# State-space stage of a two-layer hybrid backbone: both directions' decay weights in one matrix, and another order of the blocks

## The reference

```python
def ssd_chunked(x, dt, A, B, C, init_state):
    ...
    acum = jnp.moveaxis(jnp.cumsum(dtc * A.reshape(G, HG), axis=2), 2, -1)
    causal = jnp.tril(jnp.ones((CHUNK, CHUNK), dtype=bool))
    seg = jnp.where(causal, acum[..., :, None] - acum[..., None, :], -jnp.inf)
    cb = jnp.einsum('bcign,bcjgn->bcgij', Cc, Bc)
    w_intra = cb[:, :, :, None] * jnp.exp(seg)
    dtx = xc * dtc[..., None]
    y_diag = jnp.einsum('bcghij,bcjghp->bcighp', w_intra, dtx)
    decay_to_end = jnp.exp(acum[..., -1:] - acum)
    chunk_states = jnp.einsum('bcghj,bcjgn,bcjghp->bcghpn', decay_to_end, Bc, dtx)
    ...
    y_off = jnp.einsum('bcign,bcghpn,bcghi->bcighp', Cc, S_in, jnp.exp(acum))
    y = (y_diag + y_off).reshape(b, L, SSD_HEADS, P)

    y_f, s_f = ssd_chunked(x, dt_f, A[0], B, C, init_f)
    y_b, s_b = ssd_chunked(x[:, ::-1], dt_b[:, ::-1], A[1], B[:, ::-1], C[:, ::-1], init_b)
    y = y_f + y_b[:, ::-1] + p['d_skip'].astype(jnp.float32)[:, None] * x.astype(jnp.float32)
```

## Time and profile before

| | us |
|---|---|
| median of 3 runs | 1587.03 (1586.55 to 1587.52) |
| the profiled execution | 1585.54 |
| its span in the profile | 1583.6 |
| PE busy | 1487.9 (94%) |
| DVE busy | 893.6 (56%) |
| ACT busy | 673.6 (43%) |
| POOL busy | 157.0 (10%) |

### The profile page before, as it was taken

How to read it: one execution, slowest core, us unless ns; L and a number is a source line. 1 busy time by engine, 2 the same in 40 slices (tenths; PEclk the granted TensorE clock), 3 DMA queues, 4 the chain that set the end, 5 groups by cost and what they waited for, 6 DMA issues and landing times.

```text
span 1583.6 us, 21312 instructions
## 1 busy us (share of the span) xinstructions
PE 1487.9 (94%) x8503; PEld 1355.5 (86%) x8503; DVE 893.6 (56%) x1453; ACT 673.6 (43%) x1148; POOL 157.0 (10%) x141
## 2 busy tenths in 40 slices
PE   6889798899999999999998897999999999999998
PEld 2779576888899999999987896777888999999997
DVE  2697354465456654554546974455644667555562
ACT  2534453435354533342435444445335455344351
POOL 0010200344000000000010102015320010000000
PEclk9899899999999999999999998999999999999999
DMA  9446563222334556565645341221324333433430
GB/s 322 149 133 213 158 204 94 67 85 76 108 119 135 171 186 202 166 221 173 211 152 159 94 110 54 81 67 54 115 72 139 115 120 120 132 121 121 131 121 40
DMA packets 186088, 210.21 MB, mean 133 GB/s; under 512 B 10702, under 2 KB 154374, under 8 KB 185990
## 3 DMA queue, kind: packets, MB, share of 16 engines
q1 hardware_dynamic: 185990, 208.86, 42.3%
HBM read 204.90 MB, written 3.93 MB: 132 GB/s over the span
## 4 chain that ended last, share of the span: by engine, by line
PE 84%; DVE 9%; ACT 3%; issue 2%; POOL 1%; DMA 1%; SPq 0%; DVEq 0%; ACTq 0%; POOLq 0%
PE bank L638 21%; PE bank L639 21%; PE bank L640 21%; PE y_ps L886 3%; PE bank L652 2%; PE bank L653 2%; PE bank L654 2%; DVE tb L1514 2%; DVE wlo L1418 1%; PE bank L670 1%; PE seg_ps L670 1%; PE seg_ps L776 1%; PE y_ps L908 1%; PE y_ps L895 1%; PE y_ps L792 1%
## 5 line engine op out<-in xcount | busy, mean ns | idle before, releaser
L1418 DVE TENSOR_TENSOR wlo<-raw,whi 128x1024 fp32r<-128x1024 f32 (+1 forms) x288 | 353.2, 1233 | 247.6 <-ACT whi L1049 246.2
L638 PE MATMUL bank<-ahi,whi 128*128 128x384 f32 (+1 forms) x1280 | 447.0, 349 | 6.4 <-DVE wlo L1418 6.4
L1049 ACT CAST whi<-raw 128x1024 fp32r<-128x1024 f32 (+1 forms) x288 | 296.4, 1036 | 337.0 <-PE bank L640 172.8
L639 PE MATMUL bank<-alo,whi 128*128 128x384 f32 (+1 forms) x1280 | 437.6, 342 | 0.0
L640 PE MATMUL bank<-ahi,wlo 128*128 128x384 f32 (+1 forms) x1280 | 436.9, 341 | 0.0
L638 PE MATMUL bank<-bhi,whi 128*128 128x384 f32 x768 | 262.8, 342 | 8.0 <-DVE arena_g L1623 4.7
L638 PEld LDWEIGHTS bank<-ahi,whi 128*128 128x128 f32 x1280 | 245.0, 191 | 21.2 <-issue 12.3
L639 PE MATMUL bank<-blo,whi 128*128 128x384 f32 x768 | 259.4, 338 | 0.0
L640 PE MATMUL bank<-bhi,wlo 128*128 128x384 f32 x768 | 259.4, 338 | 0.0
L639 PEld LDWEIGHTS bank<-alo,whi 128*128 128x128 f32 x1280 | 245.1, 191 | 3.2 <-issue 2.7
L640 PEld LDWEIGHTS bank<-ahi,wlo 128*128 128x128 f32 x1280 | 244.7, 191 | 0.0
(11 more groups left out here) (224 smaller groups left out, 1478.4 us busy)
## 6 DMA issues: line engine op xcount, KB each, us to landing
raw<-in_w_mlp_dram SPq DMA_DIRECT2D x128, 512.0 KB, 3.6
raw<-in_w_in_dram SPq DMA_DIRECT2D x104, 512.0 KB, 3.7
raw<-in_w_mod_dram SPq DMA_DIRECT2D x96, 512.0 KB, 6.4
raw<-in_w_ssd_o_dram SPq DMA_DIRECT2D x16, 512.0 KB, 3.4
raw<-in_w_out_dram SPq DMA_DIRECT2D x16, 512.0 KB, 3.4
raw<-in_w_pool_o_dram SPq DMA_DIRECT2D x8, 512.0 KB, 3.4
raw<-in_w_attn_o_dram SPq DMA_DIRECT2D x8, 512.0 KB, 3.4
raw<-in_w_in_dram SPq DMA_DIRECT2D x8, 256.0 KB, 3.0
```

The source lines that it names most:

```text
L638: nc.tensor.matmul(dst, uh[:, k, tm_cols(m)], hi[k0 + k], start=first and k == 0, stop=False)
L639: nc.tensor.matmul(dst, uh[:, k, tm_cols(m)], lo[k0 + k], start=False, stop=False)
L1049: nc.scalar.copy(dst, src).then_inc(hi_ready, 1)
L1418: nc.vector.tensor_tensor(rest, full, top.bitcast(F32), ALU.subtract).then_inc(lo_ready, 1)
```

## The change

One matrix per chunk and head serves both directions. Above the diagonal (and on it) it holds the forward differences, below it the backward ones. PE still makes both directions' seg matrices; ACT copies the forward one from `seg_ps` to `ew` (`seg_copy`), DVE's `pick`, a predicated copy with the new constant `after` as mask, puts the backward one over it where j > i, ACT's `seg_exp` takes one Exp, and DVE's `weigh` multiplies by `cbs`, which is now an unmasked copy. The factor dt is in the exponent: `log_slots`, the logarithm of dt with a minus, is added by six more products with the identity (at L850), so that `ydiag` multiplies `ew` by x itself, once per chunk, and `dtx_rows` goes. The backward direction's diagonal, which the one matrix lacks, goes with the skip term: `skip_columns` (DVE) makes dt_b times the diagonal of C B^T plus d_skip for each head, and `skip_rows` (POOL) multiplies x by it into `dtx`. `softplus` gets a max, a memset of `log_slots`, a second Ln on ACT and the write of `log_slots`. The order in a group changes on all four engines, and with it the slots (8 in place of 13).

```diff
-SSD_SLOTS = ((2, 1, 1, 0, 1, 0, 1, 0, 0, 1, 0, 1, 0), (1, 1, 1, 1, 1, 0, 1, 0, 0, 1, 0, 1, 0))
+SSD_SLOTS = ((2, 1, 1, 1, 1, 0, 1, 1), (1, 1, 1, 1, 1, 1, 1, 1))
```

The order of PE, and its new products:

```diff
-                    ins = nc.tensor.matmul(seg_ps[:, i // 4, tm_cols(i % 4)], adt_slots[:, tm_cols(i)], tri[i % 2], start=True, stop=True,
+                    ins = nc.tensor.matmul(seg_ps[:, i // 4, tm_cols(i % 4)], adt_slots[:, tm_cols(i)], tri[i % 2], start=True, stop=False,
+                                           skip_group_check=True)
+                    ins = nc.tensor.matmul(seg_ps[:, i // 4, tm_cols(i % 4)], log_slots[:, tm_cols(i)], ident, start=False, stop=True,
                                            skip_group_check=True)
...
+                def ydiag(g, t):
+
+                    pe.wait_ge(w_ready, (l * 2 + g) * 3 + t + 1)
+                    if t or g:
+                        pe.wait_ge(y_free, (l * 2 + g) * 3 + t)
                     for h in range(HG):
+                        ins = nc.tensor.matmul(ybank[:, h * 64:h * 64 + 64], ew[:, (g + t) % 2, h, :],
+                                               xbuf[:, t, (g * HG + h) * 64:(g * HG + h) * 64 + 64], start=h == 0, stop=h == 7,
+                                               skip_group_check=True)
...
                     transposes4(2, stage[:, 2])
-                    ydiag(g, 0, 0)
                     seg(g, 2)
                     fill(slot[2])
-                    ydiag(g, 0, 1)
+                    ydiag(g, 0)
                     state_sum(3, 2)
+                    seg(g, 3)
                     fill(slot[3])
                     state_sum(4, 1)
-                    seg(g, 3)
                     fill(slot[4])
+                    seg(g, 4)
                     state_sum(5, 0)
-                    ydiag(g, 1, 0)
-                    fill(slot[5])
+                    ydiag(g, 1)
                     pe.wait_ge(stT_ready, (l * 2 + g) * 2 + 1)
                     transposes4(6, stage[:, 0])
-                    seg(g, 4)
-                    fill(slot[6])
-                    ydiag(g, 1, 1)
+                    seg(g, 5)
                     state_sum(7, 0)
-                    fill(slot[7])
+                    fill(slot[5])
                     pe.wait_ge(stT_ready, (l * 2 + g) * 2 + 2)
                     transposes4(8, stage[:, 0])
-                    seg(g, 5)
-                    fill(slot[8])
-                    ydiag(g, 2, 0)
                     yoff(9, 1, 0, 0)
-                    fill(slot[9])
+                    fill(slot[6])
                     yoff(10, 1, 1, 3)
-                    fill(slot[10])
-                    ydiag(g, 2, 1)
+                    ydiag(g, 2)
                     yoff(11, 2, 0, 2)
-                    fill(slot[11])
+                    fill(slot[7])
                     yoff(12, 2, 1, 1)
```

ACT:

```diff
+                act.wait_ge(dt_step, l * 4 + 4)
+                nc.scalar.activation(dtw, dtm, ACT.Ln).then_inc(dt_act, 1)
...
+                def seg_copy(g, t):
+
+                    act.wait_ge(seg_done, (l * 2 + g) * 6 + 2 * t + 1)
+                    n = g * 3 + t
+                    if n >= 2:
+                        act.wait_ge(ydiag_done, l * 6 + n - 1)
+                    nc.scalar.copy(ew[:, (g + t) % 2].rearrange("p h i -> p (h i)"), seg_ps[:].rearrange("p b n -> p (b n)"))\
+                        .then_inc(seg_taken, 1)
+
+                def seg_exp(g, t):
+                    act.wait_ge(seg_taken, (l * 2 + g) * 6 + 2 * t + 2)
+                    rows = ew[:, (g + t) % 2].rearrange("p h i -> p (h i)")
+                    nc.scalar.activation(rows, rows, ACT.Exp).then_inc(exp_ready, 1)
...
+                    seg_copy(g, 0)
+                    keep(1, st[:, 0, :], st_ready, (l * 2 + g) * 2 + 1)
                     seg_exp(g, 0)
...
                     fill(slot[1])
                     keep(2, st[:, 1, :], st_ready, (l * 2 + g) * 2 + 2)
+                    seg_copy(g, 1)
+                    fill(slot[2])
+                    seg_exp(g, 1)
+                    fill(slot[3])
+                    fill(slot[4])
+                    seg_copy(g, 2)
+                    keep(5, stage[:, 0, :], stT_ready, (l * 2 + g) * 2 + 1)
+                    keep(6, stage[:, 1, :], state_staged, (l * 2 + g) * 2 + 1)
+                    keep(7, stage[:, 0, :], stT_ready, (l * 2 + g) * 2 + 2)
                     seg_exp(g, 2)
...
                     keep(8, stage[:, 2, :], state_staged, (l * 2 + g) * 2 + 2)
```

DVE:

```diff
+                    nc.vector.tensor_scalar(dtm, dta, 1.2e-38, None, ALU.max).then_inc(dt_step, 1)
+                    nc.vector.memset(log_slots, 0.0)
+                    each = lambda v, n: v.rearrange("p (i h) -> p i h", h=4).unsqueeze(2).to_broadcast([P, 24, n, 4])
+                    link(nc.vector.tensor_copy(adt_slots.rearrange("p (i s h) -> p i s h", s=8, h=4), each(adt, 8)))
+                    dve.wait_ge(dt_act, l * 4 + 4)
+                    nc.vector.tensor_scalar(log_slots.rearrange("p (i s h) -> p i s h", s=8, h=4)[:, :, 2:4, :], each(dtw, 2), -1.0,
+                                            None, ALU.mult).then_inc(adt_ready, 1)
...
+                def pick(g, t):
+
+                    dve.wait_ge(seg_taken, (l * 2 + g) * 6 + 2 * t + 1)
+                    dve.wait_ge(seg_done, (l * 2 + g) * 6 + 2 * t + 2)
+                    nc.vector.copy_predicated(ew[:, (g + t) % 2], backward.unsqueeze(1).to_broadcast([P, HG, P]),
+                                              seg_ps[:].rearrange("p b (h i) -> p (b h) i", i=P)).then_inc(seg_taken, 1)
...
+                    nc.vector.tensor_copy(cbs[:], aux[:, 0:T].rearrange("p (t n) -> p t n", t=TT)).then_inc(aux_free, 1)
                     dve.wait_ge(aux_free, (l * 2 + g) * 13 + 1)
+                    pick(g, 0)
+                    skip_columns(g)
+                    fill(slot[1])
                     weigh(g, 0)
+                    fill(slot[2])
+                    pick(g, 1)
+                    next_state(g, 3, 2, 1, 1, 3)
                     weigh(g, 1)
...
                     fill(slot[3])
                     next_state(g, 4, 1, 0, 0, 2)
-                    weigh(g, 3)
                     y_diag(g, 0)
                     fill(slot[4])
+                    y_diag(g, 1)
+                    pick(g, 2)
                     fill(slot[5])
...
+                    weigh(g, 2)
+                    y_off(g, 9, 1, 0)
                     fill(slot[6])
```

POOL:

```diff
                     spread_rows(g, 3)
+                    skip_rows(g, 0)
+                    skip_rows(g, 1)
+                    spread_rows(g, 4)
                     to_end(0, 0, 0, 4)
-                    dtx_rows(g, 1)
+                    spread_rows(g, 5)
                     to_end(1, 0, 1, 5)
...
                     skip_rows(g, 2)
```

More of the change, by code:

```diff
@@ L157 @@
 for _name, _n in (("ident", P), ("upper", P), ("lower", P), ("ones", P), ("mask1", P), ("mask2", P),
-                  ("rope", 2 * 2 * HD), ("edge", 4 * 16), ("comb", 16), ("eps", 1), ("slot", 10)):
+                  ("rope", 2 * 2 * HD), ("edge", 4 * 16), ("comb", 16), ("eps", 1), ("slot", 10), ("after", P)):
     CONST[_name] = (_c, _c + _n)
@@ L195, in constants @@
     put("edge", edge)
+    put("after", (r[:, None] > r[None, :]).astype(np.float32))
     put("eps", np.full((P, 1), EPS, np.float32))
@@ L262, in backbone_step @@
         b_tm = sb("b_tm", [P, TT, 2 * P])
-        cbs = sb("cbs", [P, 2, TT, P])
+        cbs = sb("cbs", [P, TT, P])
+        skips = sb("skips", [P, 2, TT, HG])
+        cb_diag = sb("cb_diag", [P, TT])
         cst = sb("cst", [P, CONST_COLS])
@@ L295, in backbone_step @@
         own_head = const("slot")[:, 6:10]
+        backward = const("after").bitcast(mybir.dt.int32)
         tri = (upper, lower)
@@ L324, in backbone_step @@
         adt_slots = tb[:].rearrange("p a b -> p (a b)")[:, 0:6 * P]
-        acs_part = tb[:].rearrange("p a b -> p (a b)")[:, 784:784 + 6 * P]
+        acs_part = tb[:].rearrange("p a b -> p (a b)")[:, 0:6 * P]
+        log_slots = tb[:].rearrange("p a b -> p (a b)")[:, 6 * P:12 * P]
         spread = blo_low[:].rearrange("p k t -> p (k t)")[:, 0:8 * P].rearrange("p (b h i) -> p b h i", b=2, h=4)
@@ L1300, in _ @@
                     fill(slot[0])
+                    seg_copy(g, 0)
+                    keep(1, st[:, 0, :], st_ready, (l * 2 + g) * 2 + 1)
                     seg_exp(g, 0)
-                    keep(1, st[:, 0, :], st_ready, (l * 2 + g) * 2 + 1)
-                    seg_exp(g, 1)
                     fill(slot[1])
                     keep(2, st[:, 1, :], st_ready, (l * 2 + g) * 2 + 2)
-                    seg_exp(g, 2)
[L1307 to L1311, removed]
-                    fill(slot[5])
[L1313 to L1317, removed]
+                    seg_copy(g, 1)
[7 more added lines that the diff above has]
+                    keep(7, stage[:, 0, :], stT_ready, (l * 2 + g) * 2 + 2)
+                    seg_exp(g, 2)
+                    fill(slot[5])
```

(23 more changed lines are left out.)

92 lines of the change are left out of this document (23 added, 69 removed).

## The result

| | before | after |
|---|---|---|
| median of the runs beside each other | 1586.79 (4 runs) | 1568.33 (1567.74 to 1569.3, 4 runs) |
| the profiled execution | 1585.54 | 1569.3 |
| its span | 1583.6 | 1567.3 |
| PE busy | 1487.9 | 1470.3 |

The ratio of after to before is 0.9885, with a 95% interval of 0.9868 to 0.9902: 18.5 us less, between 15.6 and 20.9. I had forecast 10.9 less, 1576.1 us, with 1570.5 to 1582.5.

The account below looks back on a forecast made before the run. PE (TensorE), busy for 94% of the span, was taken to bound the kernel. The terms -21.2 + 3.1 + 3.3 + 2.2 + 1.7 = -10.9 us led from a median of 1587.03 to 1576.1 us, range 1570.5 to 1582.5.

Parts of the forecast that it names:

- The products: State-space stage on PE: half the `ydiag` calls go, 12 calls of 1.77 us, -21.2 us.
- The waits of the stages: PE's idle time in the four group stages: 3.1 against 2.44 us (first), 2.0 against 1.59 (second), +2.2 us.
- The waits of the tail: End of a group, fillers missing: PE waits at state sum 7, transposes 8, first y-off; 0.5, 0.8, 1.25 us in first groups.
- The head of a group: Start of a group: first transposes wait 0.2 us in place of 0.8, then seg 1 waits 0.3.
- The clock: First groups: PE's clock falls in both layers, one fall more than before, +1.7 us.
- Rival 1: Stages: the clock holds, also where it fell before, 1572.7 us; chance 0.17 together with waits closing better (below 1573.5).
- Ahead of the rounds: Softplus before attention: added DVE work delays PE's start of the rounds by 1.6 us a layer, +3.3 us for both.
- The identity products: Transposed sums (L850) on PE: six more products of `log_slots` with the identity per layer, 1.65 + 1.45 = +3.1 us.

Follow-up runs that it names:

- ydiag_twice: Changed kernel with each of the 8 products of a `ydiag` call issued twice, result unchanged: 1591.37 us, ratio 1.003 to the kernel before.
- before_half: Kernel before, old order, with the backward direction's `ydiag` cut from 8 products to 1: 1578.87 us, ratio 0.9951 to the kernel before.
- pick_twice: Changed kernel with each predicated copy (`pick`) issued twice in a row: 1576.13 us, ratio 0.994 to the kernel before.
- slot_rows_late: Changed kernel with the `log_slots` memset and writes moved behind the first `pooled`, the second Ln behind ACT's kT copies: 1567.95 us, ratio 0.9884.

## Why the forecast was too high

Four traces of each kernel, cut at the same instructions of PE, give mean lengths that add up to the difference of the mean spans, 1584.2 - 1566.2 = 18.0 us:

| stretch | layer 0 | layer 1 |
|---|---|---|
| up to the first transpose before attention (0), from the z units to it (1) | -0.3 | -0.2 |
| from there to the start of the rounds | +1.2 | +1.2 |
| the rounds, up to the transposed sums | -0.4 | +0.1 |
| the sums, up to the first group | -0.5 | +1.35 |
| first group | -5.0 | -5.0 |
| second group | -5.2 | -5.2 |

Step by step:

- **The products, -21.2.** Right: 12 calls of 1.73 us, so -20.8; ydiag_twice gave it back as 21.4.
- **The waits of the stages, +2.2.** Right in kind and place, too high: +0.5 (8.5 us against 8.1). The waits of the tail were 0.29, 0.81 and 1.20 us for 0.5, 0.8 and 1.25 in the first group, and 0.29 and 0.72 for 0.5 and 1.0 in the second. The head of a group was right (0.31 and 0.17 us, taken as 0.5). Most of the miss is state sum 7, 0.21 us too high in four groups, and that y-off, 0.28 in two.
- **The clock, +1.7.** This step failed. I took the fall in one trace as a property of the place, and expected one more of them. It comes in some executions and not in others, in these traces in 2 of 8 first groups before and 2 of 8 after, so the term is 0 here. Whether the new order has more of them over many executions is open (7 of 16 first groups with the runs that keep them as they are). And the fall that I left out, ahead of the first group of layer 0, became shorter by 2.0 us in the mean (4.0 us of full clock before, 2.0 after). Rival 1, that the clock holds, had the first groups right for the single profiled execution. The Trainium skill ("TensorE: Matmul & The Clock Gate", section "A second HAM failure mode: psum-queue depth-cycling") would have had the short waits around the PSUM bank bring falls; the traces show such falls in a first group in 4 of these 16, and in none of the 16 second groups, which have waits of 0.7 us and more at that bank too.
- **Ahead of the rounds, +3.3.** Right mechanism, too high: +2.3. The memset was 0.62 us to the next instruction and not 0.8, and the write of `log_slots` has 192 columns (0.26 us), not the 384 for which I took 0.45.
- **The identity products, +3.1.** Their work is nearly as forecast, 1.5 us of full clock in layer 0 and 1.35 in layer 1, but the prediction put their effect on the clock at nothing: in layer 0 the shorter fall, 2.0 us, more than pays for them. +0.9 for both layers.
- What is left, -0.8 us for the rounds and the long stretches outside the change, is about the spread from one execution to the next (162.2 to 164.4 us to the first transpose alone, for both kernels).

Sum: -20.8 + 0.5 + 2.3 + 0.9 - 0.8 = -17.9 us, the 18.0 of the spans but for rounding, against -10.9. The four terms on the costly side were all too high, by 1.7, 1.7, 1.0 and 2.2 us, and the one large term was off by only 0.4. The range failed at its lower end: 1570.5 is the case of rival 1 with little more, so it left no room for several costs that are all smaller than taken.

## What to carry to other kernels

Halving the work of the engine that bounds a stage pays in full only if the engines behind it are made ready as well: seven eighths of the same products taken out of the old order gave 7.5 us, in the changed kernel all of them are worth 20.8. A fall of the clock in one trace is one draw: read several traces of the same kernel before it gets a term, of the variants that share the stretch too, and multiply a stretch's length by its granted clock to compare it with another. Where each cost of a change is taken with something to spare, their sum is an upper end and not a middle.

## What the runs showed of the hardware

- A predicated copy of 128x1024 fp32 from PSUM, with a broadcast mask, takes 1.30 to 1.35 us, next to 1.23 for a product of two operands of that size.
- TensorE's clock falls to half (1.2 GHz) at the same place of the same program in some executions and not in others: in a first group it cost 1.6 to 1.7 us where it fell in the kernel before and in the changed one, and 3.4 us in one trace each of before_half and pick_twice. In the stretch from the transposed sums to the first group in layer 0 it fell in every trace, for 3.4 to 4.4 us of full clock in the eight traces without the identity products and 1.7 to 3.1 in the nine with them.
- A POOL product of 128x407 fp32 took 0.87 us alone and 1.79 us beside a DVE memset and copy of 128x768, in both layers (slot_rows_late).
- fp32 products of 128x64 stand 0.108 us apart for each recorded pass at full clock (16 in 1.73 us from start to start) and 0.215 at half (16 in 3.44 us, before_half).
